# Who makes a small diagonal, and where three cache copies are issued

## The reference: one step of a decoder layer

```python
x = x + 0.5 * swiglu(rms(x), ffn1)                 # FF = 5504
h = rms(x); z = h @ w_in                           # q, k, v, u, gate_a, gate_s
A = dilated_attention(q, k, v, caches)             # 3 groups of heads, windows 128, 512, 2048
B = s5_ssm(u, state) -> gelu -> glu
x = x + (sigmoid(gate_a) * (A @ w_attn_branch) + sigmoid(gate_s) * (B @ w_ssm_branch)) @ w_out
x = x + 0.5 * swiglu(rms(x), ffn2)
# rms(x) = x * rsqrt(mean(x*x) + 1e-6) * gain
# for the samples, each K/V cache is returned moved up by one row, with the new row at its end
```

## Time and profile before

| | |
|---|---|
| median of 3 runs | 2077.59 us (2077.44 to 2078.93) |
| the profiled execution's own time | 2081.41 us |
| its span, first to last instruction | 2079.6 us |
| TensorE (PE) busy | 2066.8 us, 99% |
| VectorE (DVE) busy | 1343.4 us, 65% |
| ScalarE (ACT) busy | 986.7 us, 47% |
| GpSimd (POOL) busy | 449.4 us, 22% |
| moved by DMA | 526.47 MB, mean 253 GB/s |
| mean granted TensorE clock | 0.999 of full speed |

### The profile page before, as it was taken

One profiled execution on the slowest core, in us unless ns is written; L12 is line 12 of the kernel. 1 busy time (PEld: TensorE's weight loads), 2 busy tenths in 40 slices (PEclk: granted clock), 3 DMA queues, 4 the chain that ended last, 5 costly groups with the idle time before them and its releaser, 6 DMA issues.

```text
span 2079.6 us, 48839 instructions
## 1 busy us (share of the span) xinstructions
PE 2066.8 (99%) x19331; PEld 2050.3 (99%) x19331; DVE 1343.4 (65%) x1449; ACT 986.7 (47%) x1189; POOL 449.4 (22%) x510
## 2 busy tenths in 40 slices
PE   9999999999999999999999999999999999999999
PEld 9999999999999999999999999999999999999999
DVE  7567567775555767766768968665555555555555
ACT  6654344444444545654454365554443444434443
POOL 0686414420000206763304430110000000000000
PEclk9999999999999999999999999999999999999999
DMA  8987789997897788759959976679887888878974
GB/s 252 275 276 226 260 260 270 279 264 260 251 266 221 234 299 277 236 179 321 329 177 326 283 229 196 193 248 279 263 260 244 254 271 265 260 244 256 268 217 159
DMA packets 442478, 526.47 MB, mean 253 GB/s; under 512 B 41520, under 2 KB 423392, under 8 KB 439552
## 3 DMA queue, kind: packets, MB, share of 16 engines
q1 hardware_dynamic: 427184, 507.59, 78.7%
q0 software_dynamic: 3248, 11.62, 1.6%
q10 hardware_dynamic: 11936, 5.72, 1.4%
HBM read 506.75 MB, written 105.04 MB: 294 GB/s over the span
## 4 chain that ended last, share of the span: by engine, by line
PE 92%; DVE 3%; DMA 3%; POOL 1%; ACT 1%; issue 1%; SPq 0%; ACTq 0%; DVEq 0%; POOLq 0%
PE pa L1551 30%; PE pa L1556 29%; PE pa L1552 29%; DMA qb<-q_dram 2%; DVE w_lo L1063 1%; PE pb L1754 0%; DMA raw<-in_w_in 0%; DVE xg_lo L1080 0%; DMA raw<-in_ffn_w_up 0%; PE pb L1862 0%; PE pb L1892 0%; POOL silu_v L2175 0%; DMA out_kv_p<-k_rows 0%; ACT w_hi L665 0%; PE pa L1920 0%
## 5 line engine op out<-in xcount | busy, mean ns | idle before, releaser
L1063 DVE TENSOR_TENSOR w_lo<-raw,w_hi 128x1024 fp32r<-128x1024 f32 x735 | 930.5, 1279 | 510.5 <-ACT w_hi L665 505.7
L665 ACT ACTIVATE w_hi<-raw 128x1024 fp32r<-128x1024 f32 x735 | 767.1, 1054 | 664.1 <-PE pa L1556 552.1
L1551 PE MATMUL pa<-xg_hi,w_hi 128*128 128x264 f32 x3960 | 924.6, 278 | 0.0
L1552 PE MATMUL pa<-xg_lo,w_hi 128*128 128x264 f32 x3960 | 916.2, 276 | 0.0
L1551 PEld LDWEIGHTS pa<-xg_hi,w_hi 128*128 128x128 f32 x3960 | 748.4, 189 | 8.3 <-issue 6.3
L1552 PEld LDWEIGHTS pa<-xg_lo,w_hi 128*128 128x128 f32 x3960 | 748.6, 189 | 0.2
L1556 PE MATMUL pa<-xg_hi,w_lo 128*128 128x264 f32 x3960 | 526.5, 276 | 0.0
L1556 PEld LDWEIGHTS pa<-xg_hi,w_lo 128*128 128x128 f32 x3960 | 483.3, 189 | 0.0
L1551 PE MATMUL pa<-act_hi,w_hi 128*128 128x264 f32 x1632 | 378.4, 276 | 0.0
L1552 PE MATMUL pa<-act_lo,w_hi 128*128 128x264 f32 x1632 | 377.9, 276 | 0.0
L1552 PEld LDWEIGHTS pa<-act_lo,w_hi 128*128 128x128 f32 x1632 | 308.5, 189 | 0.0
(11 more groups left out here) (364 smaller groups left out, 1353.3 us busy)
## 6 DMA issues: line engine op xcount, KB each, us to landing
raw<-in_ffn_w_up SPq DMA_DIRECT2D x172, 512.0 KB, 6.3
raw<-in_ffn_w_gate SPq DMA_DIRECT2D x171, 512.0 KB, 5.1
out_kv_s<-in_cache_kv_w SPq DMA_DIRECT2D x165, 512.0 KB
raw<-in_ffn_w_down SPq DMA_DIRECT2D x160, 512.0 KB, 4.6
raw<-in_w_in SPq DMA_DIRECT2D x152, 512.0 KB, 5.6
raw<-in_w_out SPq DMA_DIRECT2D x32, 512.0 KB, 4.9
raw<-in_w_ssm_branch SPq DMA_DIRECT2D x16, 512.0 KB, 4.6
raw<-in_ffn_w_down SPq DMA_DIRECT2D x16, 384.0 KB, 4.0
```

What stands on the lines that cost most here:

```text
L665: act.activation(w_hi[:, slot], raw[:, slot], ACT.Copy).then_inc(hi_ready, 1)
L1063: dve.tensor_tensor(w_lo[:, slot], raw[:, slot], w_hi[:, slot].bitcast(f32), ALU.subtract).then_inc(lo_ready, 1)
L1551: pe.matmul(out, wh, in_order(hi), start=first, stop=False)
L1552: pe.matmul(out, wh, in_order(lo), start=False, stop=False)
```

## The change

Two edits.

The first takes `rstd_columns` from GpSimd's program and writes it into ScalarE's, between its work on slab 7 and that on slab 8. The three multiplications become three activations (a copy, scaled by the column). The semaphores are the same.

The second takes the three copies out of gates_a and issues them in a row after the last weight load of w_out and ahead of the first of the second feed-forward. Rows and bytes are the same.

```diff
@@ sync @@
-                        if name == "gates_a" and j == 1 and i in (2, 4, 6):
-                            shift(2, 48 + 8 * (i - 2), 16)
...
             loop(sync, PH["w_out"], w_out)
+            for row in (48, 64, 80):
+                shift(2, row, 16)
             ffn(1)
@@ scalar @@
+            def rstd_columns():
+                act.wait_ge(rstd_ready, 1)
+                for t in range(2):
+                    act.activation(ssq[:, 0, t * P:(t + 1) * P], ident[:], ACT.Copy, scale=stat[:, 6 + t:7 + t]).then_inc(ssq_ready, 1)
+                act.activation(ssq[:, 0, NT:T], ident[:].rearrange("p (b k) -> p b k", b=NS)[:, :, 0], ACT.Copy,
+                               scale=stat[:, 8:9]).then_inc(ssq_ready, 1)
...
                             if first and j == 3:
                                 first_root()
+                            if first and j == 4:
+                                rstd_columns()
@@ gpsimd @@
-            def rstd_columns():
-                pool.wait_ge(rstd_ready, 1)
-                for t in range(2):
-                    pool.tensor_scalar(ssq[:, 0, t * P:(t + 1) * P], ident[:], stat[:, 6 + t:7 + t], None, ALU.mult).then_inc(ssq_ready, 1)
-                pool.tensor_scalar(ssq[:, 0, NT:T], ident[:].rearrange("p (b k) -> p b k", b=NS)[:, :, 0], stat[:, 8:9], None,
-                                   ALU.mult).then_inc(ssq_ready, 1)
...
-            rstd_columns()
```

## The result

| | kernel before | kernel after |
|---|---|---|
| median of 22 runs each, us | 2077.39 (2075.38 to 2079.16) | 2080.48 (2078.31 to 2082.56) |
| ratio, 95% interval | | 1.0015 [1.0009, 1.0021] |
| profiled execution: own time / span, us | 2081.41 / 2079.6 | 2079.47 / 2077.7 |

The change makes the kernel 3.1 us slower, where 2.0 us of gain were forecast. That is still within 0.2%, but outside the range given. The two profiled executions say the opposite of the medians: the span after is 1.9 us *shorter*, almost what the sum for the span had said (2077.6). Why both are true is the first thing to settle, and the answer turns out to be the lesson of this case.

A forecast was written before the change was run, and what follows sets the result against it. PE, busy 99% of the span, was taken as the bound, so only its waits counted. Gains of 0.84 + 1.16 = 2.0 us took the median from 2077.59 to 2075.6 us (span 2079.6 to 2077.6); range 2074.6 to 2078.6.

The forecast's parts named there:

- First edit: Diagonal, 26 to 38 us: three columns on ScalarE take 0.84 us, ready at 29.07; 0.84 us of gain kept.
- 0.30 us at slab 8 (0.38): After the diagonal, PE waits 0.38 us at slab 8 for VectorE to move out the first gate tile.
- the 1.22 us: PE's weight loader idling before the diagonal's spreading product; expected to go entirely, with 0.84 us of it kept.
- The term of 1.16 us: gates_a, around 1028 us: PE's loader idling for the copied-out probabilities (probs_t) goes, a gain of 1.16 us.
- a copy less is 1.5 us less in the chain: gates_a: removing the copy at 995.17 from the full queue ends the chain of waits to probs_t 1.5 us earlier.
- Second edit, ahead of the feed-forward: From w_out to the second feed-forward, 1360 to 1375 us: slab 476 comes later but within its reserve, 0 us.
- The delay: Slab 476 at most 5.9 us late: 1.0 us of SP issues plus 4.9 us for three copies in the queue.
- The stated reserve of 8.5 us: Slab 476: from load landing (1365.9) and w_hi (0.98 us) to PE's need at 1375.36; 2.6 us would remain.
- run a little later for one turn of the ring: Start of second feed-forward: VectorE and ScalarE slightly late, covered by the ring of four slabs and w_out's low load.
- The burst starves PE: Rival at slabs 476 to 480: slab 476 2.3 us too late, next ring turn 2.0 us more, 2079.9 us; chance 0.10.
- landings 3 to 6 us later: Sign: loads of slabs 476 to 478 land 3 to 6 us later, ScalarE waiting, PE not idling 1370 to 1400 us.
- The signs for the diagonal and for probs_t: ssq wait gone, columns about 28.2 to 29.1 us, 0.3 us or less each; probs_t wait gone or under 0.2 us.

The follow-up runs named there:

- before_twice: The kernel before, without any edit, profiled a second time; span 2074.3 us, 5.3 us less than in its first profile.
- copies_left_out: Kernel before with the three copies of gates_a left out altogether, put nowhere; 2079.0 us, 1.0002 [0.9993, 1.0011].
- the pair in step: Profiles of the kernel after and of a repeat of the first edit alone, both starting the first probabilities product at 1024.7 us; spans 2077.7 and 2074.9 us.
- two_copies: Kernel before with two of the three copies moved ahead of the second feed-forward, the first left in gates_a; 2077.81 us, 1.0002 [0.9993, 1.0011].
- row_middle: Kernel before with the three copies moved, in a row, behind the fifth load of w_out's second pass; 2079.77 us, 1.0011 [1.0002, 1.0020].
- diag_two: Kernel after with the first copy left in gates_a and two ahead of the second feed-forward; 2076.59 us, 0.9993 [0.9984, 1.0002] against before.

## Why the prediction was wrong, point by point

**First edit: right in the trace, too much in the median.** Each step of the working came out: columns 0.87 us (0.84), no wait at the spread, 0.30 us at slab 8 (0.38). The step that failed is the silent one: the 1.22 us that it takes away were taken as being there in every execution. In the GpSimd kernels' profiles they are there in five of eight.

**Second edit, out of gates_a: wrong.** The term of 1.16 us was a wait of one execution, which the forecast itself had noted as running 3.8 us above the median. before_twice shows 0.2 us there, both profiles of the first edit alone none, and copies_left_out, which frees the queue for good, shows no gain (its interval alone would allow 1.5 us). The working (a copy less is 1.5 us less in the chain) may hold for an execution with that chain, though the chain there also passes through a second query's load (issued at 1005.73, 7.42 us) and some 7 us of VectorE's work, which the forecast left out. It can't be paid out where there is no wait.

**Second edit, ahead of the feed-forward: this is where the loss comes from.** Forecast 0 us; about 2.7 us by the pair in step, +2.65 by all runs. Two terms of that step failed.
- *The delay.* Three copies were put at 4.9 us with 322 GB/s at full share, a rate taken from a stretch of weight loads. From the place where slab 476 would have been issued (1.0 us behind w_out's last load, so 1356.01) to its start on ScalarE it is 14.5 us, against 5.3 for a landing before: 9.2 us late, not 5.9. Of these, 1.5 are SP's issues (forecast 1.0). The other 7.7 us stand where the forecast had 4.9; put down to the copies alone they are 204 GB/s, but the slow stretch up to 1368 us is in them. That the loads stand behind the copies came out: the four of slabs 476 to 479 land 13.1 us after their issue in the middle. No kernel here issues the copies on another queue, so what the order alone costs is not measured. The stated reserve of 8.5 us was right: 9.2 less 8.5 is 0.7 us, which is what PE waits for w_hi (0.88 us at its loader).
- *The reserve.* It was worked out for the slab's own path only. In VectorE's program the add of w_out's last tile stands behind w_lo of slabs 476, 477 and 478, and from there goes the chain to the mean-square product. Its reserve was 1.7 us. This costs another 1.4 to 1.6 us. The forecast's sentence that VectorE and ScalarE "run a little later for one turn of the ring" looked past it.

**The rival.** "The burst starves PE", held at one in ten, named the right place, the right point of decision (8.5 us of delay) and a time 0.6 us off the median. Its price was made up otherwise: issues of 2.07 us each (they took 0.63) and a second turn of the ring (there was none: ScalarE waits 0.4 us or less for each slab behind 476). The evidence against it, that the queue is light in w_out, was true of the loads and said nothing of how fast copies run.

**What was to show it.** The forecast named what would make it wrong: PE waiting anywhere from slab 476 on. It did. It also expected landings 3 to 6 us later; that of slab 476 was 9.2. The signs for the diagonal and for probs_t, on the other hand, came as named but for small things (the columns 0.8 us later, the large ones 0.34 us each), which shows how little signs in one profile say of the median.

**What the rate is due to** is not settled. It is shown that from 1357.5 to 1370 us the engines' share is 0.95, and that while copies run they move 170 to 197 GB/s, some 0.6 of what loads alone reach for a full share (300 to 312). A copy from memory to memory reads and writes there, but the GB/s of a stretch count it once, as the page's totals of the kernel after show:

```profile
DMA packets 442478, 526.47 MB, mean 253 GB/s; under 512 B 41520, under 2 KB 423392, under 8 KB 439552
...
HBM read 506.75 MB, written 105.04 MB: 294 GB/s over the span
```

Reads and writes together are 611.8 MB where the packets' bytes are 526.5; the difference is about the 165 copies of 0.524 MB. The Trainium skill (DMA: Bandwidth & Descriptors, section Specifications) gives a limit of about 358 GB/s to memory for each core. Counted twice, three copies would take an estimated 3 x 2 x 0.524 / 0.358 = 8.8 us by it, against the 7.7 us left for them above. As loads alone reach 366 and 375 GB/s from 8 to 14 us in the first profiles of before and after, that figure is no firm bound here, and no run separates memory from the DMA engines.

## What to carry to other kernels

A wait in one profile is a gain only if it is there in most executions: when the profiled one runs microseconds above the median, profile again before pricing it, and price a wait by how often it is there. Price a copy from memory to memory by a stretch in which such copies run, not by the bytes at the loads' rate; and when loads are late, follow each engine's program order behind them to everything that waits there, since the smallest reserve may be on another chain. Bulk copies belong one by one between the loads. Several at once cost nothing until the reserve is spent: here two in a row left no wait of PE, and three cost 2.65 us.

## What the runs showed of the hardware

- Copies from memory to memory, nearly alone on the 16 DMA engines: 170 to 197 GB/s (bytes counted once) at a share of 1.02 to 1.03. Weight loads alone in the same place: 277 to 285 GB/s at 0.90 to 0.95.
- One load between two such copies, which also spreads the three issues over 8.5 us, brings the longest wait for a landing from 6.66 to 1.10 us.
- GpSimd's small 128x8 operation takes 0.31 or 1.38 us, by whether it starts 0.16 or 0.07 us ahead of a VectorE operation on two SBUF inputs, and 1.04 us where it starts inside one. This makes a wait of PE of 1.2 us come and go between executions of one kernel.
- PE's granted clock, full (2.4 GHz) for nearly all of the span, drops to half (1.2 GHz) behind PE's 3.2 us wait in some executions and not in others (not in before_twice, two_copies, row_middle and diag_two, whose spans are 2073.8 to 2074.8 us; in the other ten, of 2074.9 us and more, it does). The mean over 30 us is then 0.94 or 0.89, so about 1.8 or 3.3 us are lost (30 us times what is missing), or nothing. The wait itself is 3.2 us in all of them. Steps of this size between executions of one kernel are nearly as large as the effect studied here.
